# Half the level products of a gated recurrence, fp32 memory projections, and row sums moved between engines

## The reference, cut to what matters

```python
def memory_kv(mem, gain, w_mk, w_mv):
    h = rmsnorm(mem, gain)
    mk = (h @ w_mk).reshape(b, N_MEM, MEM_HEADS, MEM_HEAD_DIM)
    mv = (h @ w_mv).reshape(b, N_MEM, MEM_HEADS, MEM_HEAD_DIM)
...
cum = jnp.cumsum(gc, axis=1)
o_inter = jnp.einsum('blhk,bhkv->blhv', qc * jnp.exp(cum), s)
diff = cum[:, :, None] - cum[:, None, :]
decay = jnp.exp(jnp.where(tri, diff, -jnp.inf))
scores = jnp.einsum('bthk,bshk,btshk->bths', qc, kc, decay)
o_intra = jnp.einsum('bths,bshv->bthv', scores, vc)
last = cum[:, -1]
s_new = jnp.exp(last)[..., None] * s + jnp.einsum(
    'bshk,bshv->bhkv', kc * jnp.exp(last[:, None] - cum), vc)
```

## Time and profile before

| what | us |
|---|---|
| median of three executions | 1728.59 |
| lowest and highest of them | 1726.11 and 1729.11 |
| the profiled execution | 1725.81 |
| its span, first to last instruction | 1723.9 |
| TensorE busy | 1659.0 |
| VectorE busy | 1180.2 |
| ScalarE busy | 805.4 |
| GpSimd busy | 34.6 |
| recurrence, first diagonal product to first output projection | 411.74 to 717.31 |

### The profile page before, as it was taken

The page is one execution under the profiler, slowest core; times in us unless marked ns, Lnnn a source line. Parts: engine busy times, 40 slices in busy tenths (PEclk is TensorE's granted clock), DMA queues, the critical chain, the costliest instruction groups (busy, mean ns, idle before and its releaser), DMA issues.

```text
span 1723.9 us, 26838 instructions
## 1 busy us (share of the span) xinstructions
PE 1659.0 (96%) x10590; PEld 1480.3 (86%) x10590; DVE 1180.2 (68%) x1745; ACT 805.4 (47%) x1277; POOL 34.6 (2%) x49
## 2 busy tenths in 40 slices
PE   9999999999999998999998989999999999999998
PEld 8877777888999988888987889999999978888886
DVE  6477877675858589655345696665666786767686
ACT  5587777763434356413255453333332433333344
POOL 1000000000000001100000000000000000000001
PEclk9999999999999999899999999999999999999999
DMA  5232121201102142440253223333333953434332
GB/s 193 77 86 76 53 79 50 79 25 39 38 27 65 43 163 76 172 174 27 74 137 96 88 72 141 141 141 141 141 141 134 332 194 126 156 134 159 122 98 110
DMA packets 157694, 190.50 MB, mean 111 GB/s; under 512 B 5505, under 2 KB 117761, under 8 KB 155522
## 3 DMA queue, kind: packets, MB, share of 16 engines
q1 hardware_dynamic: 157570, 188.79, 33.3%
HBM read 134.58 MB, written 54.20 MB: 110 GB/s over the span
## 4 chain that ended last, share of the span: by engine, by line
PE 44%; DVE 4%; ACT 2%; issue 2%; DMA 1%; POOL 0%; DVEq 0%; ACTq 0%; POOLq 0%; SPq 0%
PE PS L2760 6%; PE PS L2762 6%; PE PS L2761 6%; PE PS L2581 6%; PE PS L2577 6%; PE PS L2579 6%; PE PS L1925 1%; PE PS L1924 1%; PE PS L1923 1%; PE PS L583 1%; DVE sbuf_gg_X L2849 1%; PE PS L2459 1%; PE PS L2461 1%; PE PS L2460 1%; PE PS L2025 0%
## 5 line engine op out<-in xcount | busy, mean ns | idle before, releaser
L621 PE MATMUL PS<-sbuf_h_hi,sbuf_w_hi 128*128 128x384 f32 x600 | 211.9, 353 | 6.0 <-ACT sbuf_g_N L632 2.7
L623 PE MATMUL PS<-sbuf_h_hi,sbuf_w_lo 128*128 128x384 f32 x600 | 201.8, 336 | 0.0
L622 PE MATMUL PS<-sbuf_h_lo,sbuf_w_hi 128*128 128x384 f32 x600 | 201.7, 336 | 0.0
L2760 PE MATMUL PS<-sbuf_ops_w,sbuf_go_u 128*128 128x512 f32 x448 | 175.2, 391 | 3.3 <-DVE sbuf_gg_X L2849 3.3
L2761 PE MATMUL PS<-sbuf_ops_w,sbuf_go_u 128*128 128x512 f32 x448 | 174.4, 389 | 0.0
L2762 PE MATMUL PS<-sbuf_ops_w,sbuf_go_u 128*128 128x512 f32 x448 | 174.3, 389 | 0.0
L2577 PE MATMUL PS<-sbuf_ops_S,sbuf_ops_w 128*128 128x288 f32 x512 | 150.9, 295 | 3.3 <-DVE sbuf_ops_S L2438 1.3
L2581 PE MATMUL PS<-sbuf_ops_S,sbuf_ops_w 128*128 128x288 f32 x512 | 151.1, 295 | 0.0
L2579 PE MATMUL PS<-sbuf_ops_S,sbuf_ops_w 128*128 128x288 f32 x512 | 150.7, 294 | 0.0
L621 PEld LDWEIGHTS PS<-sbuf_h_hi,sbuf_w_hi 128*128 128x128 f32 x600 | 113.3, 189 | 16.2 <-issue 10.0
L2602 ACT ACTIVATE sbuf_ff_u<-PS 128x576 f32<-128x576 f32 x64 | 41.6, 649 | 172.0 <-DMA uD<-sbuf_ff_sums 100.2
(11 more groups left out here) (324 smaller groups left out, 3920.0 us busy)
## 6 DMA issues: line engine op xcount, KB each, us to landing
sbuf_gg_u<-uD SPq DMA_DIRECT2D x28, 1024.0 KB, 5.2
uD<-sbuf_ff_u SPq DMA_DIRECT2D x16, 1152.0 KB, 4.2
sbuf_ff_raw<-w_ffn SPq DMA_DIRECT2D x16, 1024.0 KB, 6.2
sbuf_gg_B<-w_ffn SPq DMA_DIRECT2D x16, 1024.0 KB, 8.1
sbuf_raw<-w_in SPq DMA_DIRECT2D x28, 512.0 KB, 4.8
uD<-sbuf_ff_sums SPq DMA_DIRECT2D x16, 768.0 KB, 6.2
sbuf_X<-x_prompt SPq DMA_DIRECT2D x16, 512.0 KB, 7.3
xD<-sbuf_X SPq DMA_DIRECT2D x9, 512.0 KB, 2.6
```

Source lines behind the costliest of these rows:

```text
L621: pe.matmul(out, hi, h_hi[:, kb, tok], start=kb == 0, stop=False)
L622: pe.matmul(out, hi, h_lo[:, kb, tok], start=False, stop=False)
L623: last = pe.matmul(out, lo, h_hi[:, kb, tok], start=False, stop=kb == KB - 1)
L2760: pe.matmul(out, u_hi, x_hi, start=first, stop=False, skip_group_check=True)
```

## The change

- **Paired tiles.** A level leaves one half of each factor unused: the queries of the first blocks and the keys of the second. Now an even tile sits in the first use and the odd tile behind it, with its frames in reversed order, in the other, so that one product serves two tiles: `slots(n)` is 5 for levels 1 to 4 and 4 for levels 5 to 7. Keys and values of the odd tiles are kept reversed (`turned`, two copies instead of one), queries and decays are read with a step of -1.
- The masks are symmetrical now; `pick` collects each level in one copy into a new use of `g_S`, and `spread` copies upper, reversed lower and sample part into `g_A` once a head. Level 0 stays as it was in number (`diagonals`). `g_S` is cleared with one more memset at the start.
- **Memory projection in fp32.** `mem_kv` does one fp32 product where it did three of fp32r. Tokens lose their low part; `mem_weights` on ScalarE copies a weight unit in two halves, and VectorE no longer cuts it.
- **Row squares.** VectorE adds them (`row_square_sum`, in `last_fill` 6 and 7 and behind the levels), GpSimd no longer does.
- The gate's Exp and Ln on ScalarE move from level 5 to levels 6 and 7.
- The mask table has 12 planes instead of 8.

```diff
+    lvl = np.zeros((P, MASKS, P), np.float32)
     lvl[:, 0] = p == f
     for n, m in enumerate(LEVELS):
-        lvl[:, n + 1] = (p // (2 * m) == f // (2 * m)) & (p % (2 * m) < m) & (f % (2 * m) >= m)
+        lvl[:, n + 1] = (p // (2 * m) == f // (2 * m)) & (p // m != f // m)
+    lvl[:, MASK_ODD] = p + f == P - 1
+    lvl[:, MASK_UP] = p < f
+    lvl[:, MASK_BACK] = p + f > P - 1
+    lvl[:, MASK_16] = (p < f) & (p // NQ == f // NQ)
     return cst, lvl
...
 
-        def copy_group(act, s, use, g, index, bank, dst, scale):
+        def copy_group(act, s, use, g, index, bank, dst, scale, turned=False):
             if g == 2:
                 projected(act, use, s)
             else:
                 act.wait_ge(grp, 2 * index + g + 1)
+            if turned:
+                out, x = (y.rearrange("p (t c) -> p t c", c=P) for y in (dst[:, g * TG:(g + 1) * TG], PS[:, bank, 0:TG]))
+                act.activation(out[:, (g + 1) % 2:3:2, :], x[:, (g + 1) % 2:3:2, ::-1], ACT.Copy, scale=scale)
+                act.activation(out[:, g % 2:3:2, :], x[:, g % 2:3:2, :], ACT.Copy, scale=scale).then_inc(gev, 1)
+                return
             act.activation(dst[:, g * TG:(g + 1) * TG], PS[:, bank, 0:TG], ACT.Copy, scale=scale).then_inc(gev, 1)
...
+        NPK = 3 + NLV + 1
         LASTH = HG_HEADS - 1
 
         def lcols(n):
             return T if n == 0 or LEVELS[n - 1] < NQ else SEQ
 
-        def last_chunk(n):
-            return max(c for c, x in enumerate(lchunks) if x[0] == n)
+        def tiles_in(x):
+            return x[:].rearrange("p (t c) -> p t c", c=P)
+
+        def slots(n):
+            return 5 if LEVELS[n - 1] < NQ else 4
+
+        def level_bank(n):
+            return 2 * (n % 2)
+
+        def level_out(n):
+            b = level_bank(n)
+            return PS[:, b:b + 2, :].rearrange("p a c -> p (a c)")[:, 0:slots(n) * P]\
+                .rearrange("p (s c) -> p s c", c=P)
...
                 out = PS[:, 4 + j % 2, 0:NMEM]
                 for kb in range(KB):
-                    hi, lo = w_hi[s][:, kb * P:(kb + 1) * P], w_lo[s][:, kb * P:(kb + 1) * P]
-                    pe.matmul(out, hi, mem_h(h_hi, kb), start=kb == 0, stop=False)
-                    pe.matmul(out, hi, mem_h(h_lo, kb), start=False, stop=False)
-                    last = pe.matmul(out, lo, mem_h(h_hi, kb), start=False, stop=kb == KB - 1)
+                    w = mem_w[s][:, kb * P:(kb + 1) * P]
+                    last = pe.matmul(out, w, mem_h(r_hi, kb), start=kb == 0, stop=kb == KB - 1)
                 last.then_inc(slot_free[s], 1)
...
+                    for j in range(4):
+                        t = 2 * j + odd
+                        last = pe.matmul(PS[:, odd, j * P:(j + 1) * P], g_kT[:, t * P:(t + 1) * P],
+                                         query_of(h)[:, t * P:(t + 1) * P], start=True, stop=True)
+                    last.then_inc(G["lvl"], 1)
+                if h == LASTH:
+                    pe.wait_ge(G["i"], h * 3 + 3)
+                    pe.wait_ge(G["sout"], h)
+                pe.matmul(PS[:, 3, 0:P], g_kT[:, SEQ:T], query_of(h)[:, SEQ:T], start=True, stop=True)\
+                  .then_inc(G["lvl"], 1)
+                for n in range(1, NLV + 1):
+                    fill()
+                    if h == LASTH:
+                        last_fill(n)
+                    if h and n == 2:
+                        hg_means(pe, h - 1, 4)
+                    pe.wait_ge(G["ql"], h * NLV + n)
+                    if n > 1:
+                        pe.wait_ge(G["pred"], h * NPK + 1 + n)
+                    for j in range(slots(n)):
+                        if n == 1 and j == 4:
+                            pe.wait_ge(G["pred"], h * NPK + 3)
+                        cols = slice(j * P, (j + 1) * P)
+                        last = pe.matmul(level_out(n)[:, j, :], g_KL[:, cols], g_QL[:, cols], start=True, stop=True)
                     last.then_inc(G["lvl"], 1)
                 fill(2)
                 if h == LASTH:
...
                     act.wait_ge(G["tr"], 6 * h)
-                step(g_kT[:], g_F[:], ACT.Exp, "k")
+                act.activation(tiles_in(g_kT)[:, 1:SMP:2, :], tiles_in(g_F)[:, 1:SMP:2, ::-1], ACT.Exp)
+                step(tiles_in(g_kT)[:, 0:NT:2, :], tiles_in(g_F)[:, 0:NT:2, :], ACT.Exp, "k")
 
...
 
+            def mem_weights(act, c, s):
+
+                k, n = unit(c, s)
+                act.wait_ge(landed[s % 2], n * 16 + 16)
+                act.wait_ge(slot_free[s], k + 1)
+                w = mem_w[s]
+                act.activation(w[:, 0:512], raw[s % 2][:, 0:512], ACT.Copy).then_inc(cut_hi[s % 2], 1)
+                act.activation(w[:, 512:1024], raw[s % 2][:, 512:1024], ACT.Copy).then_inc(cut_lo[s % 2], 1)
+
             def mem_evict(j):
...
                     if h and n == 2:
                         hg_root(act, h - 1, 4)
+                    if n == 6:
+                        act.wait_ge(G["gcap"], h + 1)
+                        step(g_E[:], g_E[:], ACT.Exp, "gln", scale=-1.0)
+                    if n == 7:
+                        act.wait_ge(G["gln"], h * 2 + 1)
+                        step(g_E[:], g_E[:], ACT.Ln, "gln", bias=1.0)
                     if h == LASTH:
                         last_fill(n)
-                    if n == 5:
-                        act.wait_ge(G["gcap"], h + 1)
...
-                d, q, k = (halves(x[:], n) for x in (g_D, query_of(h), g_kT))
...
                         dve.wait_ge(G["o"], 2 * h)
-                dve.tensor_tensor(halves(g_QL[:], n)[:, :, 1, :], q[:, :, 1, :], d[:, :, 1, :], ALU.mult)
-                dve.tensor_tensor(halves(g_KL[:], n)[:, :, 0, :], k[:, :, 0, :], d[:, :, 0, :], ALU.mult)\
+                ns = slots(n)
+                d, q, k = (split(tiles_in(x)[:, 0:2 * ns - 1:2, :]) for x in (g_D, query_of(h), g_kT))
+                ql, kl = (split(tiles_in(x)[:, 0:ns, :]) for x in (g_QL, g_KL))
+                dve.tensor_tensor(ql[:, :, :, 1, :], q[:, :, :, 1, :], d[:, :, :, 1, :], ALU.mult)
+                dve.tensor_tensor(kl[:, :, :, 0, :], k[:, :, :, 0, :], d[:, :, :, 0, :], ALU.mult)
+                d, q = (split(tiles_in(x)[:, 1:SMP:2, ::-1]) for x in (g_D, query_of(h)))
+                k = split(tiles_in(g_kT)[:, 1:SMP:2, :])
+                dve.tensor_tensor(ql[:, 0:4, :, 0, :], q[:, :, :, 0, :], d[:, :, :, 0, :], ALU.mult)
+                dve.tensor_tensor(kl[:, 0:4, :, 1, :], k[:, :, :, 1, :], d[:, :, :, 1, :], ALU.mult)\
                    .then_inc(G["ql"], 1)
...
-                    dve.copy_predicated(g_A[:, t0:t0 + nt, :], lvl[:, n, :].unsqueeze(1).broadcast_to([P, nt, P]),
-                                        PS[:, c % 4, 0:nt * P].rearrange("p (t c) -> p t c", c=P))\
-                       .then_inc(G["pred"], 1)
+                dve.wait_ge(G["lvl"], h * NL + 3 + n)
+                if n > 1:
+                    dve.wait_ge(G["pred"], h * NPK + 2 + n)
+                masked(g_S[:, 0:slots(n), :], n, level_out(n))
+
+            def spread(h):
+
+                dve.wait_ge(G["pred"], h * NPK + NPK - 1)
+                for tiles, mask, x in ((slice(0, SMP, 2), MASK_UP, g_S[:, 0:4, :]),
+                                       (slice(1, SMP, 2), MASK_BACK, g_S[:, 0:4, ::-1]),
+                                       (slice(SMP, NT), MASK_16, g_S[:, 4:5, :])):
+                    out = g_A[:, tiles, :]
+                    ins = dve.copy_predicated(out, lvl[:, mask, :].unsqueeze(1).broadcast_to([P, out.shape[1], P]), x)
+                ins.then_inc(G["pred"], 1)
...
                 ins.then_inc(G["kdarg"], 1)
+                if h < LASTH:
+                    spread(h)
                 dve.wait_ge(G["kdexp"], h + 1)
-                dve.tensor_tensor(g_kT[:], g_kT[:], g_D[:], ALU.mult).then_inc(G["kd"], 1)
+                k, d = tiles_in(g_kT), tiles_in(g_D)
+                dve.tensor_tensor(k[:, 0:NT:2, :], k[:, 0:NT:2, :], d[:, 0:NT:2, :], ALU.mult)
+                dve.tensor_tensor(k[:, 1:SMP:2, :], k[:, 1:SMP:2, :], d[:, 1:SMP:2, ::-1], ALU.mult).then_inc(G["kd"], 1)
 
...
                                          h_hi[:, k, :].bitcast(F32), ALU.mult, ALU.subtract).then_inc(M["lr"], 1)
+
+            def row_square_sum(k):
+
+                dve.wait_ge(M["sq1"], k + 1)
+                if k > 1:
+                    dve.wait_ge(M["sqa"], k - 1)
+                dve.tensor_tensor(m_sq[:], m_sq[:], m_sq2[:], ALU.add).then_inc(M["sqa"], 1)
 
...
                                                  ALU.mult, ALU.mult).then_inc(M["xn"], 1)
-                if n == 3:
-                    cut_lo_unit(dve, unit(R_MEM, 0), 0)
-                    for t in range(2):
-                        for half_ in range(2):
-                            dve.wait_ge(M["hi"], 2 * t + half_ + 1)
-                            dve.tensor_tensor(mem_half(h_lo, t, half_),
-                                              PS[:, 4 + 2 * t + half_, :].rearrange("p (k c) -> p k c", k=4),
```

(13 more changed lines are left out.)

112 lines of the change are left out of this document (53 added, 59 removed).

## The result

The changed kernel takes **1707.19 us** (median of four runs, 1706.93 to 1707.87); before it took 1727.35 beside it. The ratio is 0.9885, with a 95% interval of 0.9868 to 0.9903. Forecast were 1709.6 and a range of 1702 to 1719. The profiled execution took 1707.34 with a span of 1705.5, against 1725.81 and 1723.9: 18.4 us of span are gone where the sum said 19.0. By the medians it is 20.2. A second series of the same kernel gave 1707.73 (1703.99 to 1708.5).

The account below looks back on a forecast made before the run. TensorE was taken to bound heads 0 to 2, VectorE head 3. Gains 4.2 + 4.8 + 4.8 + 5.2 = 19.0 us from 1725.81 give 1706.8; with the runs' median 2.8 above, 1709.6, range 1702 to 1719.

Parts of the forecast that it names:

- Tiles, 0.214 each on TensorE: Recurrence levels: 32 tiles a head instead of 60, 0.214 us each, TensorE 6.0 us less per head, 24.0 in all.
- Factors 1.48 a level: VectorE in each level: four factor operations instead of two take 1.48 us against 1.34, 0.14 more, 1.0 a head.
- Negative steps at no cost: VectorE's reversed-column operations: no cost, by the scan row; upper end twice the time of each reversed operation.
- (c): Rival, VectorE: reversed operands at half rate, 0.67 more a level, 1.2 more a head; 1719 us, chance 0.09.
- (d): Rival, VectorE: reversed operands at a third of the rate, slower than before; 1736 us at three times, chance 0.04.
- Heads 1 and 2: Recurrence heads 1 and 2: 6.0 less 0.4 at levels 6 and 7 and 0.8 at the end, 4.8 us gained each.
- rival (b): Recurrence levels: decay, factors and copies, not TensorE, pace every level; 3 of 6.0 a head remain; 1716.6 us, chance 0.12.
- Memset, 1.2: Start of head 0: one more memset in VectorE's chain of waits, 1.2 us of it on TensorE's path.
- rival (a): TensorE's clock in head 3: one more fall to the half clock loses 3 to 4 us; 1713 us, chance 0.13.
- Memory products: Head 3: fp32 costs 0.43 a block against 0.36, TensorE 4.5 us more; VectorE loses eight cuts and four low parts.
- 6.0 us of stretching: Head 3: removing GpSimd's three adds of squares frees VectorE of 1.05 + 2.5 + 2.5 us; its own adds cost 3.8.
- Head 3 as a sum: Head 3: TensorE's work -1.5, waits of 2.8 and some 3.0 gone, 1.0 and 1.1 given back: 5.2 us gained.

Follow-up runs that it names:

- e4: Changed kernel with the first four products of each level done twice, so 60 level products a head again: 1721.89 us, ratio 0.9972 to the kernel before.
- e6: Changed kernel with the two 256-column factors reading queries and decays forward instead of reversed: 1704.75 us, ratio 0.9872 to the kernel before.
- e8: Changed kernel with the gate's two ScalarE activations back at level 5: 1715.41 us, ratio 0.9939 to the kernel before.
- e1: Changed kernel with the new g_S memset moved from the head of VectorE's chain into a later idle time: 1703.78 us, ratio 0.9868 to the kernel before.
- e5: Changed kernel with memory products as three of fp32r again, with weight cuts and token low parts on VectorE: 1716.03 us, ratio 0.9934 to the kernel before.
- e9: Changed kernel with three fp32r memory products and their cuts, and GpSimd adding the squares, leaving the paired levels: 1714.55 us, ratio 0.9932 to the kernel before.
- e3: Changed kernel with GpSimd adding the row squares again instead of VectorE: 1702.55 us, ratio 0.9864 to the kernel before.
- e0_again: The changed kernel unaltered, run a second time: 1707.73 us, ratio 0.9884 to the kernel before.
- e2: Changed kernel with VectorE capping the first gate before any memset, the memsets moved into its waits: 1702.04 us, ratio 0.9856 to the kernel before.
- e7: Changed kernel with the first gate capped before the memsets and head 3's last sum of squares ahead of the spread: 1701.43 us, ratio 0.9851 to the kernel before.
- e10: Changed kernel with the first gate capped before the memsets and GpSimd adding the squares: 1700.32 us, ratio 0.9851 to the kernel before.

## Why the prediction was right or wrong

*Tiles, 0.214 each on TensorE:* right in size and in heads 0 to 2, where 5.0 to 5.6 of the 6.0 a head show (e4). In head 3, where they were counted in "TensorE's own work changes by -6.0 + 4.5", they do not show as time of their own: adding them back cost nothing beyond the spread, since waits and half clock shrank with them.

*Factors 1.48 a level:* right. From start to start they take 0.41, 0.40, 0.33 and 0.34 us at level 1 of head 0. The 0.32 more a level that the forecast took from the Trainium skill, VectorE: DVE Perf Modes, section on the TRN2 errata, does not show from start to start.

*Negative steps at no cost:* right. Rivals (c) and (d) are ruled out by the 417 and 418 ns; e6 shows no gain from forward reads.

*Heads 1 and 2:* 5.7 and 4.9 for 4.8 each. That ScalarE's list just exceeds the round at levels 6 and 7 was too pessimistic: TensorE has no wait there above 0.2 us. The 0.8 at the end of the head is real: TensorE's wait for the second-to-last group's copy grew from 0.58 to 1.15 and 1.24 us, and head 2 loses 0.7 more to VectorE's state. The same 0.6 in head 0 stands in the forecast without a row; there the end of the head is 0.3 us shorter (35.3 for 35.6 from level 7 on), though level 7's four products less are 0.9, so 0.6 is lost.

*Gate activations moved:* the forecast has "this removes the tightest place at level 6" and no price. By e8 it is worth 3.0 and 2.5 us in heads 1 and 2, with a fall in each, and 1.0 in head 0 without one; 1.5 of e8's 7.7 us lie in head 3, where its order is not that of the kernel before. Without the move the shorter rounds would not have held at levels 6 and 7, so rival (b) would have come true there in part.

*Memset, 1.2:* right, 19.40 us against 18.21 from the last copy of the attention to the first group (e1), 0.3 ahead of the diagonal products and 0.9 in the wait. But it was costed without what came with the wait. The half clock came in both profiles of the changed kernel, 2.8 us more than the same head without it (78.96 against 76.12). This is rival (a), one more fall, put in head 3 by the text and found in head 0.

*Memory products:* the price of 0.43 a block is right (16 blocks from 669.77 to 676.68), and so is the 2.8 us wait that goes. Wrong is what the part is worth by itself. The forecast set 4.5 us more work against waits of 2.8 and some 3.0, and the expectation of e5 made that exchange worth 2; by e5 it is worth 8.3, nearly 7 of them in head 3, and by e9 against e3 12.0. What the step left out: beside faster levels the wait for low tokens would have been 3.7; half clock came with the waits (a loss of 12.0 us in e5's head 3 against 8.8 in e0_again's); and VectorE's arrears reach into the output projection.

*Row squares:* the "6.0 us of stretching" was in the rows of before (in e3 it is 4.8, under two of the three adds), yet no gain. It counted VectorE's time in a head in which, with the cuts gone, VectorE idles 3.2 us at a time and TensorE sets the round; and VectorE's third add brought 1.9 us of wait where 1.1 was said. This part of the change gave nothing; behind level 7 of head 3 it took about 1 us.

*Head 3 as a sum:* 5.2 was forecast, 1.5 from TensorE's work and 3.7 from waits. The waits shrank by 4.0, so this much is right. The rest of the 7.0 is clock: the loss to the half clock is 2.2 us smaller than before in this profile. In the second profile of the same kernel it is as large as before, and there head 3 is 68.04, 5.3 us shorter.

*The total:* 18.4 for 19.0, and that close by luck. Against the forecast's terms head 0 with the memset came out 2.2 us worse (2.8 by the fall, with 0.6 on the good side), head 1 0.9 better, head 2 0.1, head 3 1.8 better by a smaller loss to the clock; 0.9 us were lost ahead of the recurrence, where the profiles differ anyway, and 0.3 behind it. The two effects of the clock, of which the sum has neither, nearly cancelled. The work and the waits of TensorE, on which the sum rests, were read rightly to about 1 us a head.

## What to carry to other kernels

When the engine that bounds a stretch gets faster, walk the lists of the other engines again and price each instruction that stands in front of its next hand-over: here two activations one level too early cost 3.0 and 2.5 us in heads 1 and 2. Count a saving on an engine only where that engine, after the whole change, still sets the time; and a wait of 2 to 3 us of TensorE is best removed by ordering (cap first, memsets in the waits), since it can cost its own length again in clock, 2.8 us behind the 2.9 here. Where single profiles of one kernel differ by 1.7 us in a head, look at the granted clock before a part is given the credit.

## What the runs showed of the hardware

- VectorE's fp32 products of two operands run as fast with a step of -1 as forward: 256 columns in 417 to 418 ns against 417 (420 in e6).
- With the same 2.9 us wait at the same place TensorE ran on at full clock in four profiles and at 1.2 GHz for 3.4 or 6.8 us in four. The Trainium skill, TensorE: Matmul & The Clock Gate, in the section on why this matters for kernels, says that idle gaps between bursts bring the half clock back; these runs agree, and show that one gap of this length need not. Nor is its length all: the 2.1 us wait at the start of head 3 had a fall in it or just behind it in twelve profiles of twelve, the 2.1 us wait in head 0 in neither of two.
- 28 more products in head 3 made it no longer than the spread (66.21 us against 64.89 to 68.04), with the granted clock at 0.97 for 0.87 to 0.95.
- A VectorE cap of 0.76 us takes 1.54 while GpSimd clears `g_keep` beside it (e2 at 398.35, and the same in e7 and e10); a VectorE memset of 1.02 us beside the same clearing keeps its 1.02 (the changed kernel at 399.54). These are rows, and no run tests the reason.
